# A two-layer hybrid decoder step: GpSimd's first squares wait for VectorE's fourth low half

## What is computed

```python
def rmsnorm(x, g):
    y = xf * lax.rsqrt(jnp.mean(xf * xf, axis=-1, keepdims=True) + EPS)
    return (y * g).astype(x.dtype)

def trunk_layer(x, ...):
    h = rmsnorm(x, norm1)
    qa, ka, va, hb, gate_b, gate_c, qc, fc, ic, og, zg = split_in(h @ w_in)
    # three branches: dilated window attention, gated convolution, gated recurrence
    mix = g[:, :, 0] * (ya @ w_pa) + g[:, :, 1] * (yb @ w_pb) + g[:, :, 2] * (yc @ w_pc)
    x = x + mix.astype(x.dtype) @ w_o
    h2 = rmsnorm(x, norm2)
    x = x + jnp.square(jax.nn.relu(h2 @ w_up)) @ w_down
```

## Time and profile before

| | us |
|---|---|
| median of 3 executions | 814.34 (814.22 to 814.75) |
| the profiled execution | 814.41 |
| its span, first to last instruction | 812.6 |
| TensorE busy | 803.2 (99%) |
| VectorE busy | 559.7 (69%) |
| ScalarE busy | 437.9 (54%) |
| GpSimd busy | 271.8 (33%) |

### The profile page before, as it was taken

How to read it: one execution, slowest core, us unless ns; L and a number is a source line. 1 busy time by engine, 2 the same in 40 slices (tenths; PEclk the granted TensorE clock), 3 DMA queues, 4 the chain that set the end, 5 groups by cost and what they waited for, 6 DMA issues and landing times.

```text
span 812.6 us, 17682 instructions
## 1 busy us (share of the span) xinstructions
PE 803.2 (99%) x6786; PEld 790.5 (97%) x6786; DVE 559.7 (69%) x776; ACT 437.9 (54%) x625; POOL 271.8 (33%) x246
## 2 busy tenths in 40 slices
PE   8999999999999999999999999999999999999996
PEld 8999999999999999999999999999999999999996
DVE  7979777577867665554577777866787766645552
ACT  6654566545557664444354637675455666644442
POOL 3597293055700000122139825902664000001220
PEclk9999999999999999999999999999999999999998
DMA  9898899678566688767559969987765767787761
GB/s 313 236 318 295 295 262 314 188 235 318 185 210 220 219 276 291 259 238 251 187 169 232 358 212 343 262 246 232 269 221 178 252 230 251 238 284 242 250 206 53
DMA packets 171033, 199.88 MB, mean 246 GB/s; under 512 B 19680, under 2 KB 168624, under 8 KB 169648
## 3 DMA queue, kind: packets, MB, share of 16 engines
q1 hardware_dynamic: 169040, 196.48, 74.6%
q10 hardware_dynamic: 1936, 2.61, 0.9%
HBM read 191.17 MB, written 51.90 MB: 299 GB/s over the span
## 4 chain that ended last, share of the span: by engine, by line
PE 92%; POOL 3%; DVE 3%; ACT 0%; issue 0%; ACTq 0%; DVEq 0%; POOLq 0%
PE main L690 28%; PE main L691 27%; PE main L692 27%; PE small L692 1%; PE small L691 1%; PE small L690 1%; PE small L706 1%; POOL k_lv L1738 1%; POOL cum_f L1747 1%; DVE w_lo L1270 1%; PE small L735 1%; POOL suf_f L1744 1%; PE small L749 1%; DVE h_lo L1286 0%; POOL v_cache L1728 0%; PE small L782 0%
## 5 line engine op out<-in xcount | busy, mean ns | idle before, releaser
L1025 ACT ACTIVATE w_hi<-raw 128x1024 fp32r<-128x1024 f32 (+1 forms) x256 | 266.4, 1042 | 237.7 <-PE main L692 152.9
L1270 DVE TENSOR_TENSOR w_lo<-raw,w_hi 128x1024 fp32r<-128x1024 f32 (+1 forms) x256 | 330.7, 1293 | 65.5 <-ACT w_hi L1025 64.3
L690 PE MATMUL main<-h_hi,w_hi 128*128 128x264 f32 x1248 | 358.6, 287 | 0.1
L691 PE MATMUL main<-h_lo,w_hi 128*128 128x264 f32 x1248 | 353.7, 283 | 0.0
L692 PE MATMUL main<-h_hi,w_lo 128*128 128x264 f32 x1248 | 353.5, 283 | 0.0
L690 PEld LDWEIGHTS main<-h_hi,w_hi 128*128 128x128 f32 x1248 | 235.1, 188 | 4.0 <-issue 1.3
L691 PEld LDWEIGHTS main<-h_lo,w_hi 128*128 128x128 f32 x1248 | 235.2, 188 | 0.2
L692 PEld LDWEIGHTS main<-h_hi,w_lo 128*128 128x128 f32 x1248 | 234.0, 188 | 0.0
L690 PE MATMUL main<-a_hi,w_hi 128*128 128x264 f32 x512 | 145.3, 284 | 0.0
L691 PE MATMUL main<-a_lo,w_hi 128*128 128x264 f32 x512 | 145.0, 283 | 0.0
L692 PE MATMUL main<-a_hi,w_lo 128*128 128x264 f32 x512 | 145.0, 283 | 0.0
(11 more groups left out here) (241 smaller groups left out, 1035.9 us busy)
## 6 DMA issues: line engine op xcount, KB each, us to landing
raw<-in_w_in SPq DMA_DIRECT2D x48, 1024.0 KB, 6.4
raw<-in_w_up SPq DMA_DIRECT2D x32, 1024.0 KB, 5.3
raw<-in_w_down SPq DMA_DIRECT2D x32, 1024.0 KB, 5.4
out_kvs<-in_cache SPq DMA_DIRECT2D x48, 512.0 KB
out_kvs<-in_cache SPq DMA_DIRECT2D x32, 496.0 KB
raw<-in_w_o SPq DMA_DIRECT2D x8, 1024.0 KB, 5.8
raw<-in_w_br SPq DMA_DIRECT2D x8, 768.0 KB, 4.9
gates<-q_scratch SPq DMA_DIRECT2D x4, 768.0 KB, 8.0
```

Of the source, the lines that this page charges most:

```text
L690: pe.matmul(out[:, 0:TOK], wh, rh, start=start and k == 0, stop=False)
L691: pe.matmul(out[:, 0:TOK], wh, rl, start=False, stop=False)
L1025: act.activation(w_hi[:, slot(l, u), 0:k, :], raw_of(u, k), ACT.Copy).then_inc(w_hi_ready, 1)
L1270: dve.tensor_tensor(w_lo[:, slot(l, u), 0:k, :], raw_of(u, k), w_hi[:, slot(l, u), 0:k, :].bitcast(F32), ALU.subtract).then_inc(w_lo_ready, 1)
```

## The change

One wait is added on GpSimd, ahead of the wait for the input's first quarter. `h_ready` counts the low halves that VectorE has written.

```diff
             pool.memset(ones, 1.0).then_inc(ones_set, 1)
+            pool.wait_ge(h_ready, 4)
             for k in range(4):
                 pool.wait_ge(x_in[k // 2], 16)
                 ins = pool.tensor_tensor(square_of(k), x[:, k, :], x[:, k, :], ALU.mult)
             pool_start(ins)
             pool_start(pool.tensor_tensor(sq_sum[:, :], square_of(0), square_of(1), ALU.add))
```

## The result

The changed kernel takes 816.09 us (median of 12 executions, 815.56 to 816.56), the kernel before 814.54 (12 executions on the same chips, 814.22 to 815.38): **1.55 us slower, ratio 1.0018 with a 95% interval of 1.0010 to 1.0026**. The lowest of the twelve are 815.56 and 814.22, 1.34 apart. The profiled execution took 816.16 us with a span of 814.3; the span of before was 812.6.

What follows compares the result with a forecast made beforehand. The prediction took TensorE as the bound, fed late by VectorE in the head; 0.87 us later at the fourth piece's last matmuls plus 0.10 for restarting gave 814.34 + 0.97 = 815.3 us, range 814.5 to 816.1.

Steps and rivals of the forecast that it cites:

- What bounds the kernel: TensorE bounds nearly everything behind the head; what it loses or gains in the head goes one for one to the end.
- What is removed: Up to VectorE's fourth h_lo, three GpSimd instructions no longer stand in its way: 1.20 us earlier, 0.50 us left after idling.
- What is moved: GpSimd starts at about 7.13; its seven instructions then alternate with VectorE's until the fourth piece's w_lo ends at 13.84.
- the turns: In the head, GpSimd and VectorE alternate, each end following the last: w_lo 0.55, h_lo 0.29, square 0.48, add 0.61 us.
- the upper bound: At about 7.71 to 7.76 GpSimd's second square goes ahead of VectorE's w_lo: last w_lo at 14.04, or +1.17 us.
- the point from which the row starts: End of GpSimd's first square, run alone for 0.63 us, put at 7.76; from there the engines alternate.
- What TensorE makes of it: 1.19 us ahead at the third piece, then new waits: fourth piece's last matmuls +0.87, restart +0.10, sum +0.97 us.
- What is covered: Behind the fourth piece, the fifth w_lo (by 1.4 us), late squares, GpSimd's sum (4.1 us early) and weight loads cost nothing.
- VectorE is not held up at the new place: Rival: GpSimd's instructions slip between VectorE's behind 7.7 us; -1.28 us, 813.1; 3 in 100.
- Little change: Rival: one or two GpSimd instructions fall into unseen gaps of VectorE; 0 to +0.6 us, 814.3 to 814.9; 12 in 100.
- The clock: Rival: thinned TensorE work from 9.3 to 13.9 lowers the granted clock, costing 2 us more, 817.3; 5 in 100.
- The wait did hold GpSimd back: Answers the rival that the wait ahead of GpSimd's first square holds nothing back; 814.3; 1 in 100.

Runs made afterwards that it cites:

- after_plus1: The changed kernel with one square more on GpSimd, behind the first, into sq_sum (overwritten later); 816.05 us, ratio 1.0018 to the kernel before.
- after_again: The changed kernel itself, unchanged, profiled once more; 816.07 us (one execution), beside 814.74 for the kernel before.
- late_w_after: The changed kernel with one square more on ScalarE ahead of its first w_hi; 815.89 us, ratio 1.0018 to the kernel before.
- the fills: The kernel before with fills that read nothing in place of GpSimd's squares and adds in the head; 813.64 us, ratio 0.9989.
- fills_wait4_again: The changed kernel with fills in place of GpSimd's squares and adds, profiled a second time; 816.17 us (one execution), beside 814.61 for the kernel before.
- fills_wait4: The changed kernel, wait for four kept, with fills in place of GpSimd's squares and adds; 814.20 us, ratio 0.9996 to the kernel before.
- wait_8: The changed kernel with GpSimd's squares waiting for eight low halves instead of four; 815.65 us, ratio 1.0010 to the kernel before.

## Why the prediction was right, and where its size was off

**What bounds the kernel.** Held. The head passes its lateness on one for one: 796.0 to 796.5 us from the sum of squares to the end in seven profiles.

**What is removed.** Held: the first w_lo and the next two h_lo ran at 0.69 and 0.89 for two, and VectorE then idled for the second w_hi (0.34 us for a forecast 0.63; 0.66 in after_plus1, at the forecast's landing).

**What is moved.** In the profile of after the turns held to 0.01 us in their sum, and so did their order; in after_again and late_w_after the order was that of the upper bound, which the prediction priced at 0.20 us more and which costs 0.15 (12.66 for 12.49 and 12.53). The term that was mis-sized is the point from which the row starts: put at 7.76, measured 8.21. Of the 0.45 us, 0.38 came from the landing of the first weights in the one profile of before, the earliest of all that were taken (w_hi at 4.95; the others lie from 4.97 to 5.62), the rest from small terms such as a hand-over of 0.08 for the 0.05 put down. The step that failed is reading a start that hangs on a DMA from a single profile, as though it were fixed. The other side of the difference was read from the same profile: before starts its row from the second quarter of the input, and that landed earliest there, too. after_plus1, which has one square more and landed at 4.97, had its first square at 7.21 and the sum at 17.46, for 7.13 and 17.38.

**What TensorE makes of it.** Held in kind: two waits on w_lo, one on h_lo, the stop at the second w_lo gone, the last four matmuls of the fourth piece 0.05 us behind their w_lo, 0.1 for the restart. In size 1.33 + 0.10 instead of 0.87 + 0.10, all from the start of the row. The lead at the third piece was put at 1.19 us and was 0.52 (9.97 for 10.49), as TensorE's first piece itself began later with the late w_hi (6.65 for 6.21); in after_plus1 the third piece starts at 9.40, 1.09 ahead. As forecast, all of it is taken back by the fourth w_lo.

**What is covered.** The late squares, the fifth w_lo and GpSimd's sum cost nothing, as forecast. One of these readings was off without harm: the fifth w_lo was put 1.14 us behind the fourth, which is a distance of starts; from end to end it is 1.37 in before and after alike, so it ended at 15.67 and not at 14.98, and TensorE asked for it at 16.90. The loads of weights behind the head, costed at nothing, are not always covered: in the profile of after a w_hi waited 0.8 us for the DMA of a later pair and TensorE 0.43 us for ScalarE at 34 us (L706). In the three other profiles with the wait and the squares this is missing.

The two medians lie 1.55 apart, the lowest executions 1.34 and the medians of the profiled heads 1.31. Of the changed kernel's twelve executions the five with a mean granted clock of 0.995 took 816.13 to 816.56 us, the seven at 0.996 and 0.997 took 815.56 to 816.16, and all four profiles with the wait and the squares are at 0.997. What those slower executions lost, and whether it has to do with the change, was not profiled and stays open.

**The rivals.** That VectorE is not held up at the new place fell with the alternating ends. Little change (0 to +0.6) fell too. The clock stayed at 1.00 in the head of every profile, also in after, where TensorE was busy for only 2.50 of the 3.50 us from 11.0 to 14.5. The wait did hold GpSimd back. The Trainium skill's rule ("SBUF — State Buffer", Who interferes with whom) that a GpSimd instruction that only writes doesn't contend is borne out by the fills, with w_lo at 0.69 beside them. Its rule that the order of issue decides is borne out at 7.79, where VectorE asked just ahead of the extra square of after_plus1 (7.80) and ran first, and by after_again, where GpSimd's second square started at 8.45, before VectorE asked at 8.72, and ran first.

**The range.** It held the median by 0.01 us (816.09 for an upper end of 816.1), and that is luck: the measured +1.55 lies above the +0.6 to +1.3 to which the forecast gave 78 in 100, and the range only reached so far because it was drawn wider than that. The mechanism was right, the size 0.6 us short. The band was made from the turns' uncertainty, and not from that of the landings, which turned out the larger.

## What to carry to other kernels

Two engines whose ends alternate as here pay in turns: an instruction of the one on the critical path waits for one instruction of the other, however many are queued there. Delaying the other engine only helps if its work lands where the first is idle or ahead. Here VectorE gave way five times before, partly where it was ahead anyway, and seven times in the profile after, all on the path; taking four of GpSimd's seven instructions off it was worth 1 us. And where a forecast starts from a DMA's landing, look at more than one profile, or give the range the spread of landings; find out for each of the two kernels which landing it is that its head hangs on, as it need not be the same one.

## What the runs showed of the hardware that was not expected

- The alternation itself was forecast, but not how exact it is: 13 turns in a row within 0.01 us of the sum of single prices, 0.48 us for a 128x264 square of GpSimd, 0.61 for its add, 0.29 for VectorE's 128x264 and 0.55 for its 128x512. A 128x1024 w_lo of VectorE was a turn of 1.08 us, and which engine started its row a few tenths earlier decided whether GpSimd's key product had to sit it out (59 us, fills_wait4_again).
- The landing of the same first load of weights moved between 4.95 and 5.62 us over the profiles, with nothing changed ahead of it, and the start of the square that waits for the second quarter of the input between 5.31 and 6.04.
- One idle time of TensorE of 1.57 us in the recurrence was followed by 3.3 us at a granted clock of 0.50, in both profiles of fills_wait4 (1.56 and 0.51 in the first), though TensorE had work throughout that stretch. One of 1.76 us in the head of wait_8 was followed by a clock of 1.00. What decides between the two no run here shows.
